# Two gate tiles as a twelfth block pair, and six attention steps without a slice of projection

## The reference

```
z = x @ w_in                      # 6416 columns: GLA q,k,v,r; rank-16 gate; SWA q,k,v; memory q; 3 x 1024 merge gates
o_a = GLA linear attention        # 4 heads of 128
o_b = sliding-window attention    # 8 query heads, 2 kv heads of 64, window 128, softmax with a sink
o_c = softmax attention into 256 memory tokens   # 4 heads of 128
mix = (sigmoid(g_a) * (o_a @ w_br_gla) + sigmoid(g_b) * (o_b @ w_br_swa) + sigmoid(g_c) * (o_c @ w_br_mem)) @ w_o
x = LN1(ALPHA * x + mix);  x = LN2(ALPHA * x + ConvFFN(x))
```

## Time and profile before

| | us |
|---|---|
| median of three runs | 1750.6 |
| profiled execution, its own time | 1747.55 |
| its span, first to last instruction | 1745.4 |
| block pairs, about | 43 to 271 |
| attention steps, about | 560 to 763 |
| busy in the span: TensorE, VectorE, ScalarE, GpSimd | 1722.2, 1088.5, 757.8, 219.0 |
| DMA traffic | 207.84 MB |

### The profile page before, as it was taken

How to read it: one execution, slowest core, us unless ns; L and a number is a source line. 1 busy time by engine, 2 the same in 40 slices (tenths; PEclk the granted TensorE clock), 3 DMA queues, 4 the chain that set the end, 5 groups by cost and what they waited for, 6 DMA issues and landing times.

```text
span 1745.4 us, 31878 instructions
## 1 busy us (share of the span) xinstructions
PE 1722.2 (99%) x12185; PEld 1667.6 (96%) x12185; DVE 1088.5 (62%) x1556; ACT 757.8 (43%) x1366; POOL 219.0 (13%) x319
## 2 busy tenths in 40 slices
PE   9999999999999999999999999999999999999997
PEld 8999999999998899899998889999999999999997
DVE  6644432666645766566664788777777777554474
ACT  6433332445434555563340255444455444433342
POOL 0000000000001200000000033333333331002011
PEclk9999999999999999999999999999999999999999
DMA  5333328422436311125463232222222213875672
GB/s 165 111 109 109 122 77 256 117 71 76 138 93 206 105 46 49 52 90 147 141 203 96 80 85 85 86 73 73 73 73 74 87 58 130 269 250 171 210 234 72
DMA packets 191505, 207.84 MB, mean 119 GB/s; under 512 B 21525, under 2 KB 152406, under 8 KB 191414
## 3 DMA queue, kind: packets, MB, share of 16 engines
q1 hardware_dynamic: 189558, 200.60, 36.9%
q0 software_dynamic: 1856, 5.99, 1.0%
HBM read 157.43 MB, written 48.53 MB: 118 GB/s over the span
## 4 chain that ended last, share of the span: by engine, by line
PE 65%; DVE 3%; issue 1%; SPq 1%; DMA 1%; ACT 1%; POOL 0%; ACTq 0%; POOLq 0%; DVEq 0%
PE banks L1681 24%; PE banks L1179 10%; PE banks L1180 10%; PE banks L1181 10%; PE banks L1638 5%; PE banks L1475 1%; PE banks L1492 1%; PE banks L1487 1%; PE banks L1455 1%; PE banks L1460 1%; DMA kpad<-gates_scratch 1%; PE banks L1649 0%; DVE wo L2809 0%; PE banks L1615 0%; SPq L797 0%
## 5 line engine op out<-in xcount | busy, mean ns | idle before, releaser
L1681 PE MATMUL banks<-x_free_r,a_hi 128*128 128x256 f32 x1232 | 226.8, 282 | 0.8 <-DVE a_lo L2919 0.5
L1179 PE MATMUL banks<-act_hi,w_hi 128*128 128x352 f32 (+1 forms) x672 | 223.7, 333 | 2.3 <-DVE w_lo L2448 1.4
L1181 PE MATMUL banks<-act_hi,w_lo 128*128 128x352 f32 (+1 forms) x672 | 218.0, 324 | 0.0
L1180 PE MATMUL banks<-act_lo,w_hi 128*128 128x352 f32 (+1 forms) x672 | 217.9, 324 | 0.0
L1681 PEld LDWEIGHTS banks<-x_free_r,a_hi 128*128 128x128 f32 x1232 | 190.1, 188 | 1.3 <-DVE x_free_r L2945 0.7
L1681 PE MATMUL banks<-xs_hi,a_hi 128*128 128x274 f32 x616 | 178.8, 290 | 1.7 <-DVE xs_lo L2945 1.1
L1681 PE MATMUL banks<-xs_lo,a_hi 128*128 128x274 f32 x616 | 178.4, 290 | 0.0
L1681 PE MATMUL banks<-xs_hi,a_lo 128*128 128x274 f32 x616 | 178.3, 289 | 0.0
L1681 PE MATMUL banks<-x_free_r,a_lo 128*128 128x256 f32 x616 | 173.4, 281 | 0.0
L1180 PE MATMUL banks<-h_lo,w_hi 128*128 128x384 f32 (+1 forms) x448 | 147.3, 329 | 0.0
L1179 PE MATMUL banks<-h_hi,w_hi 128*128 128x384 f32 (+1 forms) x448 | 146.8, 328 | 0.0
(11 more groups left out here) (355 smaller groups left out, 4324.0 us busy)
## 6 DMA issues: line engine op xcount, KB each, us to landing
w_raw<-in_w_down SPq DMA_DIRECT2D x112, 256.0 KB, 3.5
w_raw<-in_w_in SPq DMA_DIRECT2D x80, 256.0 KB, 3.9
gate_in<-gates_scratch SPq DMA_DIRECT2D x24, 529.0 KB, 3.6
h_keep<-conv SPq DMA_DIRECT2D x22, 530.0 KB, 2.7
gates_scratch<-zu SPq DMA_DIRECT2D x11, 1058.0 KB, 7.1
w_raw<-in_w_up SPq DMA_DIRECT2D x44, 256.0 KB, 3.9
x_free<-in_w_up SPq DMA_DIRECT2D x44, 256.0 KB, 3.7
h_raw<-h_keep SPq DMA_DIRECT2D x22, 384.0 KB, 5.2
```

The costliest lines, as they stand in the source:

```text
L1179: pe.matmul(out, hi, b_hi, start=start, stop=False)
L1180: pe.matmul(out, hi, b_lo, start=False, stop=False)
L1181: return pe.matmul(out, lo, b_hi, start=False, stop=stop)
L1681: last = pe.matmul(out, a[j][:, k, :], x[s][j][:, k, :], start=fresh and k == 0 and n_ == 0, stop=k == 3 and n_ == 2, skip_group_check=True)
```

## The change

NZ becomes 12: gates 22 and 23 are made by a twelfth block pair (an odd one, so the last pair now uses the other banks and `z_raw_b`). The attention keeps gates 16 to 21, 6 tiles and 18 slices. The table `ATT_FILL` lists the steps that have a slice; the six steps of `ATT_BARE` have none. In a bare step VectorE copies the turned probabilities of unit k before it normalises unit k + 1, and ScalarE copies them before the exponentials of unit k + 1 (at the end of the step before). Splits of weight tiles follow each tile's third slice, wherever that now falls, and the middle of the attention is written out on three engines in place of the loop.

```diff
-NZ = 11
+NZ = 12
+Z_LAST = (NZ - 1) % 2
-Z_GATES = (12, 14, 6, 8)
+Z_GATES = (12, 14, 6, 8, 22)
+ATT_BARE = ((0, 5), (1, 2), (1, 5), (2, 2), (2, 5), (3, 2))
+ATT_FILL = [(i, j) for i in range(5) for j in range(6) if (0, 3) <= (i, j) <= (4, 2) and (i, j) not in ATT_BARE]
...
-T_MERGE = T_MQ + 18
-T_WO = T_MQ + 30
-T_FFN = T_MQ + 38
+T_MERGE = T_MQ + 16
+T_WO = T_MQ + 28
+T_FFN = T_MQ + 36
...
+    def att_fill(i, j):
+        return ATT_FILL.index((i, j)) if (i, j) in ATT_FILL else None
...
-        last = gate_loop(T_GATE_B // 2, 16, 4, gate_st2, PS_GATE_B)
+        last = gate_loop(T_GATE_B // 2, 16, 3, gate_st2, PS_GATE_B)
...
-        with pe.Fori(1, NZ // 2) as i:
+        with pe.Fori(1, (NZ - 1) // 2) as i:
             z_pair(i * 2, 0)
             z_pair(i * 2 + 1, 1)
-        z_pair(NZ - 1, 0)
+        z_pair(NZ - 2, 0)
+        z_pair(NZ - 1, Z_LAST)
...
-            proj_slice(PS_Z + gi, 3 + 4 * (gi % 2), 0, gi)
+            proj_slice(PS_Z + gi, bank_a(1 - Z_LAST, gi % 2), 0, gi)
...
         def gate_slice_b(i, j, beside=None):
 
-            if j % 3 == 0:
-                tile_start(i + (T_GATE_B // 2 + j // 3 - 1), 1 - j // 3)
-            proj_slice(i * 6 + (PS_GATE_B + j - 3), (PS_GATE_B + j - 3) % 2, 1 - j // 3, j % 3, beside)
+            s = att_fill(i, j)
+            if s is None:
+                return
+            f = s // 3
+            if s % 3 == 0:
+                tile_start((T_GATE_B + f) // 2, f % 2)
+            proj_slice(PS_GATE_B + s, (PS_GATE_B + s) % 2, f % 2, s % 3, beside)
...
         att_steps(0, True, False)
-        with pe.Fori(1, NT // 2 - 1) as i:
+        for i in range(1, NT // 2 - 1):
             att_steps(i, False, False)
...
+        def next_gate(i, j):
+            s = att_fill(i, j)
+            if (i, j) == (0, 2):
+                split_hi(T_GATE_B // 2, 1)
+            elif s is not None and s % 3 == 2:
+                split_hi((T_GATE_B + s // 3 + 2) // 2, s // 3 % 2)
...
-                probs_out(k, P)
+                if (i, j) not in ATT_BARE:
+                    probs_out(k, P)
...
                 values_out(k, j % 3, c, w)
-                if j % 3 == 2:
-                    split_hi(i + (T_GATE_B // 2 + b), 1 - b)
+                next_gate(i, j)
+                if (i, j + 1) in ATT_BARE:
+                    probs_out(k + 1, P)
                 n = j + 2
                 w, nk = (DEC, P + DEC) if last and j >= 4 else (P, 2 * P)
                 exp_unit(k + 2, i * 4 + (n - n // 3), n % 3, n % 2, w, nk)
...
+                if (i, j) in ATT_BARE:
+                    probs_out(k, P)
                 if not (first and j == 1):
                     normalise(k + 1, i * 4 + (n - n // 3), n % 3, n % 2, w, nk)
-                if not (first and j < 2):
+                if not (first and j < 2) and (i, j) not in ATT_BARE:
                     probs_out(k, P)
...
-                if j % 3 == 2:
-                    split_lo(i + (T_GATE_B // 2 + j // 3), 1 - j // 3)
+                s = att_fill(i, j)
+                if (i, j) == (0, 2):
+                    split_lo(T_GATE_B // 2, 1)
+                elif s is not None and s % 3 == 2:
+                    split_lo((T_GATE_B + s // 3 + 2) // 2, s // 3 % 2)
```

More of the change, by code:

```diff
@@ L475, in program @@
     BRANCHES = (2, 0, 1)
-    PS_Z, PS_G, PS_GA, PS_FILL, PS_MQ, PS_MQ_B, PS_MK, PS_MV, PS_GATE_B, PS_END = 6, 9, 11, 15, 57, 60, 63, 65, 67, 91
+    PS_Z, PS_G, PS_GA, PS_FILL, PS_MQ, PS_MQ_B, PS_MK, PS_MV, PS_GATE_B, PS_END = 6, 9, 11, 15, 57, 60, 63, 65, 67, 85
     q = Semaphores(sem)
@@ L568, in raw_count @@
         if par:
-            return 384 if isinstance(c, int) and c < 2 else c * 32 + 352
+            return 448 if isinstance(c, int) and c < 2 else c * 32 + 416
         return 32 * (W0 + 1) if isinstance(c, int) and c < 2 else c * 16 + 32 * (W0 + 1)
@@ L851, in _ @@
         merge_tile(T_MERGE // 2, 1, BRANCHES[1], 0)
-        last(3, (0,))
+        last(2, (0,))
         sp.wait_ge(q.staged, 2 * NT + 2)
@@ L855, in _ @@
         gate_back(0)
-        last(3, (1,))
+        last(2, (1,))
         for s in range(3):
-            sp.wait_ge(gate_stored[s], 16 * (10 + NFILL))
+            sp.wait_ge(gate_stored[s], 16 * (8 + NFILL))
         for k in range(12):
@@ L1917, in _ @@
         z_window(1, 1)
-        with act.Fori(1, NZ // 2) as i:
+        with act.Fori(1, (NZ - 1) // 2) as i:
             z_window(i * 2, 0)
             z_window(i * 2 + 1, 1)
+        z_window(NZ - 2, 0)
         for k in range(3):
             for s in range(2):
-                z_snap(NZ - 1, 0, s, k)
+                z_snap(NZ - 1, Z_LAST, s, k)
         split_hi(1, 0, used=(q.prod_mm[1], z_count(NZ - 1, 0)))
         for s in range(2):
-            z_snap(NZ - 1, 0, s, 3)
+            z_snap(NZ - 1, Z_LAST, s, 3)
         split_hi(1, 1, used=(q.prod_mm[1], z_count(NZ - 1, 4)))
@@ L1937, in _ @@
         for gi in range(3):
-            gate_out(PS_Z + gi, 3 + 4 * (gi % 2), gi, gate_st, 0)
+            gate_out(PS_Z + gi, bank_a(1 - Z_LAST, gi % 2), gi, gate_st, 0)
             if gi == 1:
@@ L2079, in gate_out_b @@
         def gate_out_b(i, j):
-            gate_out(i * 6 + (PS_GATE_B + j - 3), (PS_GATE_B + j - 3) % 2, j % 3, gate_st2, i * 2 + (1 + NFILL + j // 3))
+            s = att_fill(i, j)
+            if s is not None:
+                gate_out(PS_GATE_B + s, (PS_GATE_B + s) % 2, s % 3, gate_st2, 2 + NFILL + s // 3)
+        def next_gate(i, j):
[4 more added lines that the diff above has]
+                split_hi((T_GATE_B + s // 3 + 2) // 2, s // 3 % 2)
         def att_steps(i, first, last):
@@ L2109, in _ @@
         att_steps(0, True, False)
-        with act.Fori(1, NT // 2 - 1) as i:
+        for i in range(1, NT // 2 - 1):
             att_steps(i, False, False)
@@ L2161, in _ @@
         for gi in range(3):
-            act.wait_ge(gate_stored[gi], 16 * (10 + NFILL))
+            act.wait_ge(gate_stored[gi], 16 * (8 + NFILL))
         act.wait_ge(q.k_turned, 1)
@@ L2571, in _ @@
         z_window(1, 1)
-        with dve.Fori(1, NZ // 2) as i:
+        with dve.Fori(1, (NZ - 1) // 2) as i:
             z_window(i * 2, 0)
             z_window(i * 2 + 1, 1)
+        z_window(NZ - 2, 0)
         for k in range(3):
             for s in range(2):
-                z_combine(NZ - 1, 0, s, k)
+                z_combine(NZ - 1, Z_LAST, s, k)
             if k == 0:
@@ L2793, in _ @@
         att_steps(0, True, False)
-        with dve.Fori(1, NT // 2 - 1) as i:
+        for i in range(1, NT // 2 - 1):
             att_steps(i, False, False)
```

## The result

| | before | after |
|---|---|---|
| median | 1751.45 us (6 runs, 1750.44 to 1754.89) | 1765.06 us (6 runs, 1761.55 to 1768.21) |
| profiled execution | 1747.55 us, span 1745.4 | 1761.55 us, span 1759.4 |
| ratio after / before | | 1.0076, 95% interval 1.0060 to 1.0092 |

The change makes the kernel slower by about 13.3 us (0.0076 x 1751), where 9.9 us was predicted. The forecast time was 1760.5 us, the range 1756 to 1765. By the ratio the changed kernel takes 1.0076 x 1750.6 = 1763.9 us, inside the range; its own median, 1765.06, lies at the upper end of it. The kind of result and most of its terms came as worked out, the size is 3 to 4 us short. The two profiled executions are 14.0 us apart.

A forecast was written before the change was run, and what follows sets the result against it. TensorE was taken as the bound, with hand-overs to VectorE and ScalarE limiting the bare steps. The pair's +20.64 us less 10.72 saved in the attention gave +9.9: 1760.5 us on the median, range 1756 to 1765.

The forecast's parts named there:

- The pair, +20.64: Twelfth block pair in the steady part: 168 matmuls without a gap, costing 20.64 us.
- A': Attention step of kind 0 in the next group of three, following a bare step; its values were to wait 1.58 us.
- C steps: Attention steps of kind 2 (memory), all six bare ones among them; each bare one was to wait 0.48 us for VectorE's copy.
- B': Attention step of kind 1 in the next group; normalised before the copy of A', with no wait expected in it.
- The chain of 14.95 us: Hand-overs from S to the values of A', none shortened by the missing slice; a bare step therefore saves 1.93 us, not 3.99.
- S: Start on TensorE of the scores of A', computed in the step before the bare one; the chain is counted from it.
- The cycles with a weight split: Bare steps (1,5) and (3,2), with the next tile's weight split in the step before: each saves 1.68 us.
- the sample's: Step (3,0), after bare step (2,5), where ScalarE first empties the sample's keys: 1.57 us saved.
- The clock: Rival, 3%: TensorE falls to 1.2 GHz in bare steps, giving 1773 to 1785 us; the forecast itself had nothing for it.
- nothing saved: Rival, 5%: the copy falls behind VectorE's other work in every bare step; +20.6 us, 1771.2 us.
- only C waits: Rival, 4%: only the bare steps wait, 0.48 x 6 = 2.9 us, and A' nothing; 1750.2 us, no change.
- Everything hidden: Rival, 4%: VectorE's order doesn't bind and the six slices are pure gain; -3.3 us, 1747.3 us.

The follow-up runs named there:

- experiment 1: The changed kernel with the pair kept, each bare step computing an unused slice again and all copies in the old order: ratio 1.0104, 1769.94 us.
- experiment 4: The changed kernel with VectorE's copy in the bare steps back behind the normalisation, ScalarE's half still early: ratio 1.0177, 1781.54 us.
- experiment 3: The changed kernel with VectorE copying the turned probabilities first also in the step after each bare one: ratio 1.0022, 1753.87 us.
- experiment 5: The changed kernel with GpSimd's staging started only after the values of step A' instead of after the scores of step C: ratio 1.0054, 1759.04 us.
- experiment 7: The changed kernel with copies first also after bare steps, the weights' low part later, the sample's keys copied earlier, staging not delayed: ratio 0.9988, 1747.91 us.
- experiment 8: The kernel of experiment 5 with three needless VectorE reciprocals ahead of the scalings of B' in (1,0), (1,3) and (2,3): ratio 1.0085, 1765.81 us.
- experiments 2: The changed kernel with unused matmuls, 1 to 12, on TensorE ahead of each wait of a bare step and the step after it: ratio 1.0057, 1762.06 us.

## Why the prediction was right, and what it had too small

- *The result as a whole:* the mechanism was right, a chain of hand-overs that leaves a bare step 2 of its 4 us. The range held it narrowly, and in part by luck: its upper end had been set for the near ends of the rivals, not for the clock, and errors the other way took 0.8 us off.
- *The pair, +20.64:* 20.65 in the trace, and experiment 1 agrees within its interval. The attention's start moved by 21.06. Of the 0.4 us between, 1.1 arose ahead of the pairs (TensorE's first slice starts at 14.34 for 13.25; it starts anywhere from 13.25 to 14.71 in the eleven profiled executions), and 0.6 went again at the memory rows (a wait of 0.4 us for 0.9). Both vary from one execution to the next, so the 0.4 us are scatter.
- *A slice, 3.98, and its six removals:* right. 23.5 us of waits in experiment 4 are these six.
- *Waits in a bare step and its A':* their total was right, 13.0 us for 13.2, but in other parts. The wait in C steps was 0.26 us where 0.48 was worked out, 1.39 where the low part stood ahead of the copy, as the exception had it; the wait of A' was there (2.1, or 0.46 behind a 1.39). The condition on which it hung, VectorE's normalisation of B' ahead of the copy of A', is shown by experiment 3; the wait itself was 2.1 us for 1.58, for the reason under the next point (1.58 in experiment 5, without it).
- *The chain of 14.95 us:* its links were right, 14.87 in experiment 5, but for one that the change itself lengthened: GpSimd's staging starts when the scores of C are done, the missing slice brings them 3.65 us nearer to S (11.39 us behind it for 15.04), and it then falls on VectorE's scalings. I had costed each link by its duration in the old schedule and not asked what else would move beside it. 0.43 us three times, 1.3 us, is what the chain got longer than worked out.
- *The cycles with a weight split:* I had 1.68 us saved, it was 2.01; ScalarE's 0.25 us of delay did not come through. With the sample's (1.67 for 1.57) that is 0.8 us in the change's favour.
- *The clock:* the term that was mis-sized. It stood as a rival of 3% that would take all six steps to half speed and 1773 us or more, and as nothing in the forecast. It is neither: a fall comes behind some of the 2.1-us waits, costs 1.55 us where a slice follows, and ends before the next bare step. Two in the profiled execution (3.1 us); the six runs of the changed kernel go from 1761.55 us at a mean clock of 0.997 to 1768.21 at 0.993, in step with it. The row I leaned on, 1.08 us of idleness at 1.00, held only half as much idleness as the 2.06 us that I had worked out for a bare step and its A'. At the waits that I had worked out (1.58 us at most) the term would indeed have been nothing: the table has no fall at 15 waits of 1.2 to 1.6 us.

Sum of the profiled executions: 20.65 + 0.41 - 10.72 + 1.3 + 3.1 - 0.8 = 13.9 us, for 14.0 measured. Both mis-sized terms meet in one place: the staging made a wait of 1.6 us into one of 2.1, and in the table nearly all falls stand at waits of more than 2 us.

Of the rivals, "nothing saved" is what the kernel does without the early copy (experiment 4), and "only C waits" what it does with the copy first in A' (experiment 3, 1753.9 us for 1750.2: the low parts and the sample's keys are what it left out). "Everything hidden", 1747.3 us, is nearly reached by experiment 7 with 1747.9.

## What to carry to other kernels

Work taken off the engine that is the bound is only worth what the chains beside it let through: add up the hand-overs from one fixed event to the next before counting the work as gained, and move the copies that the bound waits for ahead of all that nobody waits for, in the step after the hole as well as in it. When a schedule is tightened, look for every queue that is released by an event that now comes earlier, as GpSimd's staging here, and ask beside what it will run. In this kernel a wait of TensorE of 2.07 us or more often had a price of its own in the clock: 14 of 18 such waits had a fall, and a fall cost 1.55 us more.

## What the runs showed of the hardware that I had not expected

- TensorE's granted clock fell to 1.2 GHz behind waits of about 2 us in an otherwise full stretch, not always: see the table. A fall cost 1.55 us where slices of gates came next. The spread of the runs of one kernel goes with the mean clock: 1.7 us for each 0.001 over the changed kernel's six runs (6.66 us over 0.004).
- One fall of 16 came without a wait of TensorE, during products of 32 to 128 columns (experiment 8, at 532.77).
- TensorE's wait for the memory rows, ahead of the first attention steps, is 0.3 to 2.6 us long in the profiled executions of the nine experiments, 0.4 us in that of the changed kernel and 0.9 us in that of the kernel before; what sets its length stays open.
- Four VectorE scalings of 128x256 took 1.63 to 1.68 us instead of 1.14 beside a GpSimd copy of 128x512, in the thirteen steps of four kernels (the changed one, experiments 2, 3 and 7) where the two met in full.
